# Hybrid decoder step on one core: ScalarE's norm of the next tile two heads earlier, and another order of the first loads

## What is computed

```python
xn = rms_norm(x, attn_norm_w)
q_lat, c_kv, k_pe, rq, rk, rv, rg = split(xn @ w_in)       # 1024 -> 2464 columns
...                                                        # latent attention (8 heads) beside retention (8 heads)
h = x + concat([mla_out, ret_out]) @ w_o
xb = rms_norm(h, ffn_norm_w)
q = xb @ w_peer_q                                          # 8 heads x 2 x 128
s1, s2 = q1 @ sub_keys1.T, q2 @ sub_keys2.T                # 128 scores each
# top 16 of each, top 16 of their 256 sums: 16 experts a head, 128 a token
act = gelu(einsum('nd,nhkd->nhk', xb, peer_u[experts]))
y = h + einsum('nhk,nhkd->nd', g * act, peer_v[experts])
```

## Time and profile before

| | us |
|---|---|
| median of three runs | 3798.01 (3796.01 to 3811.87) |
| the profiled execution, its own time | 3796.36 |
| its span in the trace | 3794.6 |
| PE busy (matmul) | 2526.1 (67%) |
| DVE busy | 2401.7 (63%) |
| POOL busy | 2285.2 (60%) |
| ACT busy | 416.2 (11%) |
| read from HBM | 1357.80 MB |

### The profile page before, as it was taken

The page is one execution under the profiler, slowest core; times in us unless marked ns, Lnnn a source line. Parts: engine busy times, 40 slices in busy tenths (PEclk is TensorE's granted clock), DMA queues, the critical chain, the costliest instruction groups (busy, mean ns, idle before and its releaser), DMA issues.

```text
span 3794.6 us, 35385 instructions
## 1 busy us (share of the span) xinstructions
PE 2526.1 (67%) x11810; PEld 1285.0 (34%) x11810; DVE 2401.7 (63%) x6238; ACT 416.2 (11%) x953; POOL 2285.2 (60%) x2118
## 2 busy tenths in 40 slices
PE   5746575766666666666676666667677666588683
PEld 4633133412342234323342233223343232144250
DVE  3586557664767466665776477666666476766564
ACT  1101100110001000110011000110011000032010
POOL 0055766577567755677557756676657755446636
PEclk9769887888888878888788878888799877688767
DMA  4489999999999999999999999999999999678969
GB/s 154 167 312 350 407 411 370 369 406 411 377 394 388 410 409 357 369 383 411 378 383 391 400 399 372 375 396 411 358 382 392 406 396 382 222 249 293 372 239 349
DMA packets 376009, 1366.42 MB, mean 360 GB/s; under 512 B 61074, under 2 KB 72530, under 8 KB 348178
## 3 DMA queue, kind: packets, MB, share of 16 engines
q0 software_dynamic: 304128, 1107.43, 75.4%
q1 hardware_dynamic: 71698, 256.73, 17.6%
HBM read 1357.80 MB, written 6.18 MB: 359 GB/s over the span
## 4 chain that ended last, share of the span: by engine, by line
DMA 27%; POOL 27%; PE 21%; DVE 12%; issue 12%; ACT 1%; SPq 1%; DVEq 0%; POOLq 0%; ACTq 0%
DMA v_ring<-down_rows,codesT 17%; POOL u_ring L555 14%; POOL v_ring L566 13%; PE ps L612 7%; PE ps L635 7%; DMA wbuf<-weights 6%; DMA u_ring<-up_rows,codes 4%; DVE arena L1262 3%; PE ps L791 2%; PE ps L838 2%; DVE u_ring L1292 2%; DVE root_t L1262 1%; DVE idx L1262 1%; DVE top_c L1262 1%; DVE root_y L1262 1%
## 5 line engine op out<-in xcount | busy, mean ns | idle before, releaser
L1292 DVE CUSTOM_DVE_ANT_0 u_ring<-u_ring,xn 128x1024 f32<-128x1024 f32 x1056 | 1267.5, 1221 | 794.7 <-DMA u_ring<-up_rows,codes 793.2
L612 PE MATMUL ps<-v_ring,Z 128*32 128x512 f32 x4224 | 1165.2, 764 | 810.8 <-DMA v_ring<-down_rows,codesT 583.9
L555 POOL DMA_INDIRECT u_ring<-up_rows,codes x1056 | 1166.8, 1105 | 796.1 <-issue 303.1
L566 POOL DMA_INDIRECT v_ring<-down_rows,codesT x1056 | 1117.2, 1058 | 700.7 <-PE ps L612 386.8
L612 PEld LDWEIGHTS ps<-v_ring,Z 128*32 128x32 f32 x4224 | 194.8, 124 | 1522.5 <-DMA v_ring<-down_rows,codesT 993.8
L635 PE MATMUL ps<-wbuf,xT 128*128 128x256 f32 (+1 forms) x2016 | 511.3, 417 | 222.7 <-DMA wbuf<-weights 139.0
L635 PEld LDWEIGHTS ps<-wbuf,xT 128*128 128x128 f32 (+1 forms) x2016 | 398.2, 204 | 359.5 <-issue 159.8
L791 PEld LDWEIGHTS ps<-xT,wbuf 128*128 128x128 f32 x2304 | 293.8, 208 | 112.5 <-issue 81.4
L791 PE MATMUL ps<-xT,wbuf 128*128 128x128 f32 (+1 forms) x2304 | 312.3, 294 | 28.1 <-DMA wbuf<-weights 27.2
L1089 ACT ACTIVATE arena<-arena,nb 128x128 f32<-128x128 f32 (+7 forms) x64 | 49.6, 775 | 498.0 <-DVE nb L1266 498.0
L1262 DVE MAX8 vals<-arena 128x8 f32<-128x128 f32 (+1 forms) x288 | 69.1, 281 | 51.2 <-ACT arena L1127 50.1
(11 more groups left out here) (283 smaller groups left out, 2142.4 us busy)
## 6 DMA issues: line engine op xcount, KB each, us to landing
wbuf<-weights SPq DMA_DIRECT2D x216, 1024.0 KB, 8.3
u_ring<-up_rows,codes POOLq DMA_INDIRECT x1056, 9.2
v_ring<-down_rows,codesT POOLq DMA_INDIRECT x1056, 9.2
table<-ffn_w SPq DMA_DIRECT2D x9, 512.0 KB, 6.8
resid<-x_prompt SPq DMA_DIRECT2D x8, 512.0 KB, 6.8
table<-decay_in SPq DMA_DIRECT2D x8, 512.0 KB, 10.1
y_prompt<-arena SPq DMA_DIRECT2D x8, 512.0 KB
kT<-cache_latent SPq DMA_DIRECT2D x56, 64.0 KB, 6.8
```

The costliest lines, as they stand in the source:

```text
L555: pool.indirect_dma_start(out=u_ring[:, i % U_RING, :], out_offset=None, in_=up_rows, in_offset=bass.IndirectOffsetOnAxis(ap=codes[:, of, ...
L566: pool.indirect_dma_start(out=v_ring[:, v % V_RING, :], out_offset=None, in_=down_rows, in_offset=bass.IndirectOffsetOnAxis(ap=codesT[:, t ...
L612: mm = pe.matmul(acc[32 * c:32 * c + 32, half, :], Z[:, at:at + GS], v_ring[:, v % V_RING, half * 512:(half + 1) * 512], start=False, stop ...
L1292: dve.tensor_tensor_reduce(u, u, xn[:, 1 if t == TILES else t % 2], 1.0, 0.0, ALU.mult, ALU.add, dots[:, k:k + 1]).then_inc(dot_done, 1)
```

## The change

ACT's `norm_in(t + 1)` is called at s = 4 instead of s = 6. At the head, `load_tile(0)` comes first, then `ident` and `attn_wc` on a semaphore of their own (`first_in`), then the first two weight pieces, then the other fourteen constants. PE, ACT and DVE wait for `first_in` only; DVE waits for the fourteen after its copy in the first turn of tile 0, and halves `ret_wb` there. The clears of `kT` and `vN` are dropped, and that of `R` comes behind `norm_in(0)`.

```diff
-        N_CONST = 16
+        N_CONST = 14
@@ sync
-            for dst, src in ((ident, eye), (attn_wc, attn_w), (qa_wc, qa_w),
-                             ...
-                             (place_p, place_rows), (place_s, place_new), (spread, spread_new)):
-                sp.dma_start(dst[:], src).then_inc(const_in, 16)
...
             def front(t):
-                for w in range(O_0):
+                for w in range(0 if t else 2, O_0):
                     load_piece(t, w)
...
             load_tile(0)
+            for dst, src in ((ident, eye), (attn_wc, attn_w)):
+                sp.dma_start(dst[:], src).then_inc(first_in, 16)
+            for w in range(2):
+                load_piece(0, w)
+            for dst, src in ((kva_wb, kva_w.partition_broadcast(P)), (qa_wc, qa_w),
+                             (q_wb, q_w.partition_broadcast(P)), (k_wb, k_w.partition_broadcast(P)),
+                             (ret_wb, ret_w.partition_broadcast(P)), (dec_cross, decay_cross), (dec_k, decay_k),
+                             (dec_state, decay_state), (k1T, keys1T), (k2T, keys2T), (ptab, page_table),
+                             (place_p, place_rows), (place_s, place_new), (spread, spread_new)):
+                sp.dma_start(dst[:], src).then_inc(const_in, 16)
@@ tensor
-            pe.wait_ge(const_in, 16 * N_CONST)
+            pe.wait_ge(first_in, 32)
@@ scalar, out_and_peer
-                    if s == 6 and following:
+                    if s == 4 and following:
                         norm_in(t + 1, following)
@@ scalar, main
             norm_in(0, P)
+            act.wait_ge(first_in, 32)
@@ vector, project
                 turned_copy(t, 0, n, attn_wc)
+                if t == 0:
+                    dve.wait_ge(const_in, 16 * N_CONST)
+                    dve.wait_ge(const_set, 2)
+                    do(dve.tensor_scalar, ret_wb[:], ret_wb[:], 0.5, None, ALU.mult)
@@ vector, main
-            dve.wait_ge(const_in, 16 * N_CONST)
-            dve.wait_ge(const_set, 2)
-            do(dve.tensor_scalar, ret_wb[:], ret_wb[:], 0.5, None, ALU.mult)
-            do(dve.memset, kT[:], 0.0)
-            do(dve.memset, vN[:], 0.0)
+            norm_in(0, P)
             do_signal(R_ready, 1, dve.memset, R[:], 0.0)
-            norm_in(0, P)
+            dve.wait_ge(first_in, 32)
```

More of the change, by code:

```diff
@@ L248, in page @@
             return pg[b % PG_RING][:, j * KVR:(j + 1) * KVR]
+        first_in = sem("first_in")
         const_in = sem("const_in")
```

## The result

The changed kernel takes **3762.78 us** in the median of five runs (3730.49 to 3770.93), against 3798.01 us before; the ratio is 0.9875 with a 95% interval of 0.9832 to 0.9918. The forecast was 3760 us. The profiled execution took 3750.97 us, with a span of 3749.2.

The account below looks back on a forecast made before the run. DMA engines were taken to bound the kernel once gathers run, a dependent chain its head. Head 16.5 plus sum of squares 21.5 made 38.0 us off 3796.36, 3758.4; with 1.65 for the median, 3760 us, range 3742 to 3783.

Parts of the forecast that it names:

- The bound: Once gathers run, an edit is worth the idle DMA time it fills, not the wait taken from DVE or PE.
- The head: Start of program: earlier x loads bring DVE's root from 24.37 to 7.9 us; 16.5 us passed through to the end.
- its cover of 8 us: Tile 0: DVE's 1 us wait for the other constants costs nothing, its next urgent work being near 23 us.
- The seven waits: Tiles 1 to 7: DVE's waits of about 9 us for ACT's sum vanish; top 16 of head 4 comes 5.5 us earlier.
- the packed windows: 15 us behind each wait, tiles 1 to 7: DMA work packed to a share of 1.02 gains 21.5 us together.
- it can't be done in 15 - 5.5: Tile 1, behind the wait: 11.5 us of packed DMA work limits the gain to 3.5 us instead of 5.5.
- DVE's time counts in full: Rival, tiles 1 to 7: all 38 us of DVE's earlier time reach the end, 3743.5 us; chance 0.15.
- Only the head: Rival: tiles 1 to 7 give back what they win, leaving the head's 16.5 us, 3781.5 us; chance 0.17.
- Gathers colliding with weights: Rival, tiles 1 to 7: earlier gathers delay PE's weight pieces, PE 45 us later, 3826 us; chance 0.04.
- The bytes as a floor: Rival, whole run: 358 GB/s is the core's long-run limit, so all gains are paid back, 3798 us; chance 0.04.
- rule against it: Whole run: the skill's 358 GB/s limit puts the kernel at its floor, change worth nothing; the trace's 410 leaves 13%.

Follow-up runs that it names:

- the held kernel: The change plus 28 chained DVE multiplications before the top 16 of head 4 in tiles 1 to 7; 3787.90 us, 0.9960 of the kernel before.
- the head alone: The change with the sum of squares back at s = 6; 3783.06 us, 0.9954 of the kernel before; on the slower chip 3965.50 us, 0.9974.
- the sum of squares alone: The kernel before with only the sum of squares moved to s = 4; slower chip, 3935.91 us, 0.9893 of the kernel before.
- the change again: The unaltered change run once more on the slower chip; 3934.35 us, 0.9873 of the kernel before.
- s = 5: The change with the sum of squares at s = 5 instead of s = 4; slower chip 3921.67 us, 0.9845; later set 3748.52 us, 0.9877.

## Why the prediction was right

**The bound.** "An edit is worth the idle time of the DMA engines that it fills, not the wait that it takes from DVE or PE" was too narrow. In stretch A the held kernel shows DVE's time itself to count, 37.8 us in and 41 to 44 us longer than in two traces of the change. The share of sixteen engines says how busy they were with what had been issued; in this stretch POOL issues as DVE frees buffers. It was not wrong altogether: by the sixteenth dot DVE waits for gathers again, and a third of its gain is gone.

**The head.** Forecast 16.5 us, measured 16.2 at the root and 16.8 at tile 0's `xn`, and 15 to 18 in the run time on chips of like speed, by medians that are uncertain by about 10. The table landed 5.3 us after its issue (5.0 taken). The wait for the other constants was 2.8 us instead of 1, and free, as its cover of 8 us said; the constants came later since some of SP's issues took longer than the 0.47 us taken, `place_s` 1.53. That all later steps keep their distances held.

**The seven waits.** They went, in all seven tiles, and the keys of head 4 became the next thing that is late, for 2.6 to 3.6 us, as forecast. The cost of ACT's early instruction was 1.60 - 1.16 = 0.44 us in tile 1 where I took 0.7. The top 16 came 6.0 us earlier per tile (42.2 / 7) where I had 5.5. The total of the waits for ACT's sums came to 49.4 us, not 35: a slip of mine, since 109.8 less seven waits of 9 us is 46 by its own rows.

**The term that was mis-sized** is the packed windows, 21.5 us. By the change against the head alone it is 29 us, by the held kernel some 32 (0.9960 - 0.9876 = 0.84% of 3800, between two sets), at the sixteenth dot 30, by stretch A 42. The step that failed is "it can't be done in 15 - 5.5". It took the work of a window as fixed and a share near 1 as no room. With the gathers issued earlier the same window held six or seven of them, its share was near full, and the 15 us behind it stayed at 0.95 to 1.03, so no later window paid for it. Tile 7 shows it most plainly: I gave it 0.9 us because its window stood at 0.96, and its stretch A became 7.7 us shorter, its sixteenth dot 3.9 us earlier. At 0.96 this window had moved only 350 GB/s; after the change it moved 410. Packed by bytes, 15 x (1 - GB/s / 410), the windows of the earlier trace rows, with tiles 4 to 6 again at the mean of the first three, would have given 4.8 + 4.1 + 5.5 + 14.4 + 2.2 = 31.0 us. That is worked out afterwards, from rows of the kernel before; its agreement with the 29 to 32 us is one case, and no run tested it as a rule. The rival "DVE's time counts in full", 38 us, was right for the stretch; for the run time the value lies between it and my forecast. That the total came out within 3 us of the median is partly luck: the packed term was low by 8 to 10 us, and this set's median relative to before, 35 us, lies below the 47 us that the ratio of 0.9875 gives. In the other two sets the change brought 1.27% and 1.24%, 47 to 51 us.

**The rivals.** Only the head: refuted by the head alone, 0.9954 against 0.9876. Gathers colliding with weights: PE's waits for pieces went from 139.0 to 143.2 us, where the rival needed 45 more. The bytes as a floor: the same reads now take 1357.80 MB / 3749.2 us = 362 GB/s over the span, and the gain came through, so the mean of 358 was no ceiling here. The Trainium skill, DMA: Bandwidth & Descriptors, section Specifications, has about 358 GB/s as one core's limit of HBM, worked out as 716 GB/s of a stack divided by two cores. This trace of one core doesn't agree with it as a limit, with 362 over the span and 410 in its full windows. That the row is half of a stack's figure, and so a share for two cores, my "rule against it" left out.

## What to carry to other kernels

A short instruction that stands behind others in its engine's stream, though it needs nothing of them, can hold up an engine that isn't the busiest; look at what each wait is *for*, and move the instruction ahead to a place where its engine idles. One step is enough if that step is idle. At the head of a program, order the loads by who needs them first, and keep the effects of edits apart from their sum: here 10.5 and 7.7 us made 16.2. Where an idle stretch holds up the freeing of buffers that gathers wait for, neither its own length nor the idle share of the DMA engines behind it is its value: here the length gave 42 us, the share 21.5, and the run time 29 to 32. Look how soon the engine waits for gathers again once it comes earlier; the last 3 us of each tile were worth nothing for that reason.

## What was not expected of the hardware

One chip ran the kernel before 4.9% slower (3983.67 against 3798.01 us), with a granted clock of 0.786 to 0.801 in its runs of that kernel, against 0.800 to 0.821 on the two others where it was run again. In the window from 440 to 460 us the first chip moves 410 GB/s in the kernels before and after. On the slower one the head alone and, in the same window, the sum of squares alone have:

```profile
440.00:460.00 20.00, 10.99 (x35) 2.38 (x34) 9.42 (x16) 2.11 (x3) 15.73 (x15) 0.67 0.99 375
440.00:460.00 20.00, 12.52 (x40) 2.88 (x40) 8.39 (x15) 0.38 (x1) 15.70 (x15) 0.84 1.03 410
```

The first is a full share with 9% fewer bytes, the second is as on the first chip; the change again has 358 there and s = 5 has 371. So the slowness comes and goes; over the whole span the four traces read and write 345 to 347 GB/s, against 359 before on the first chip. Their chain that ended last has a part that none of the ten traces on the other chips has, 11% to 19% of the span; here the head alone:

```profile
POOL 20%; another core or an unknown queue 19%; PE 17%; DMA 15%; issue 14%; DVE 13%; SPq 1%; ACT 1%; DVEq 0%; ACTq 0%
```

What slowed it isn't known. The ratio of the change was the same there, 0.9873, but absolute expectations made for one chip don't carry to another.
